# Gated mixer of a decoder trunk: the projection of r cut into pieces between the steps of the recurrent core

## The chip, the cores and the metric

The kernel runs on one core of a Trainium2 chip. The metric is the device time of one execution in microseconds (us). The engines are TensorE (PE, matmuls; PEld is its weight load), VectorE (DVE), ScalarE (ACT), GpSimd (POOL) and SyncE (SP), which here issues the weight transfers.

## The reference, cut to what matters

The program computes a two-layer decoder trunk on 512 tokens of width 1024. Each layer has a half feed-forward block, a token mixer, a cross attention to a fixed memory and a second half feed-forward block. The mixer of the second layer is a gated linear attention with four heads, keys of width 128 and values of width 256, in chunks of 64 tokens. The change touches this mixer alone.

```python
def gla_mixer(h, w_in, w_g2, b_g, head_norm, w_out):
    q, k, v, g_lr, r = _split(h @ w_in, ODD_SPLITS)
    gk = jax.nn.log_sigmoid((g_lr @ w_g2 + b_g)) / GLA_TAU
    ...
    q_dec = q * jnp.exp(G)
    k_inv = k * jnp.exp(-G)
    k_rem = k * jnp.exp(G_last - G)
    att = jnp.where(tril, jnp.einsum('bnhid,bnhjd->bnhij', q_dec, k_inv), 0.0)
    o_intra = jnp.einsum('bnhij,bnhjv->bnhiv', att, v)

    def step(state, xs):
        qd, kr, vv, dec = xs
        o = jnp.einsum('bhid,bhdv->bhiv', qd, state)
        state = dec[..., None] * state + jnp.einsum('bhjd,bhjv->bhdv', kr, vv)
        return state, o
    ...
    o = rmsnorm(o, head_norm).reshape(Bb, S, GLA_DV) * jax.nn.silu(r)
    return o @ w_out
```

## The kernel before, in words

All weights stream through one queue in units of 128 x 1024 elements. SyncE loads a unit into one of two raw buffers (w_raw). ScalarE copies it to the rounded high half w_hi (split_hi, L305), and VectorE subtracts to get the low half w_lo (split_lo, L310). Four slots hold split units. The order of these splits is written out by hand: behind unit u of a projection stands the split of unit u + 4 (AHEAD). A projection of one unit is 8 blocks of 3 matmuls of 512 columns (three, L325 to L327): high by high, high by low, low by high.

In the mixer (gla), TensorE projects g_lr, q, k and v, in this order. The gates are worked out on ScalarE and VectorE beside the projection of v, head by head. For each head n VectorE then forms g_q, g_kr (the keys that decay to the chunk's end, L1300) and g_k, and TensorE turns g_kr by four transposes a head (the keys' turns, L1693). ScalarE copies them out to g_krt (L834). Then TensorE projects r in 8 units. Behind each, ScalarE takes the bank through Silu into g_r (L645) and splits a coming unit, whose low half VectorE forms.

Then comes the core, 16 steps w: four groups T of 128 tokens by four heads n. A step on TensorE has these parts:

- att: 128 x 128 scores into bank w % 2 (L1725), which VectorE copies out under a mask (g_att, L1311)
- u: two products of keys and values of 64 rows each (L1731), from which VectorE updates the state g_S (L1320, L1322)
- mixed(w - 1): the output of the step before, from g_att and g_S (L1710, L1716). ScalarE copies it to f (L842) and sums its squares (L845)

At the last head of a group ScalarE takes a root (L849, it needs the Sqrt table), and VectorE's mean and normed scale the group before (L1337 to L1349). Behind the core TensorE turns f (L1742), VectorE multiplies it by g_r (gated, L1361), ScalarE and VectorE split the product (L854, L1366), and the output projection (L1492 to L1494) starts when all of it is there.

The banks of u are what decides how far TensorE may run ahead of VectorE's state updates; before the change there are two pairs of them:

```python
                        new, up = g_S[:, n, (c + 1) % 3, :], bank(2 + 4 * a + w % 2)[:, 0:GDV]
```

Of the kernel before, what the change touches and what calls it, by code (L numbers as in the profile page):

```python
# [60 lines left out]
def trunk(nc, parts, x, mem, wstream, cols, gains, post_gains, mem_gains, head_gain, w_ra, w_ri, w_g2, out):  # L61
# [7 lines left out]
    with ctx:  # L69
# [92 lines left out]
        def bank(b):  # L162
            return ps[:, b, :]
# [121 lines left out]

        def proj_bank(i, t):

            first = PT0[i, UNITS[parts[i][0]][0][0]]
            return bank(t - first if parts[i][0] in ("even", "gla") and t - first in (2, 3) else t % 2)

        VG = {"ffn": 0, "cross": 2, "even": 1, "gla": 2}
        V0 = [sum(VG[k] for k, _, _ in parts[:i]) for i in range(NP)]
# [154 lines left out]
        def _(act):  # L447
# [344 lines left out]
            def gla(i):  # L792
                nc.scalar.dma_start(g_w2[:, :], w_g2).then_inc(gs["w2_in"], 16)
                nc.scalar.dma_start(g_gain[:, :], head_gain.to_broadcast([P, GDV])).then_inc(gs["gain_in"], 16)
                act.preload_act_table_set("natural_log_exp_and_others")
                act.wait_ge(w_free, U[i, "g_lr"] + 3)
                nc.scalar.activation(g_lr[:, :], bank(PT0[i, "g_lr"] % 2)[0:GR, :], ACT.Copy).then_inc(p_free, 1)
                split_units(i, "g_lr", 1)
                project(i, "q", GH, g_q)
                for n in range(GH):  # L800
                    c = COLS["b_g"] + n
                    act.wait_ge(gs["z_full"], n + 1)
                    nc.scalar.activation(g_kr[:, n, :], bank(4 + n), ACT.Identity, bias=col[:, c:c + 1])\
                        .then_inc(gs["z"], 1)
                project(i, "k", GH, g_k)
                act.wait_ge(p_free, PT0[i, "k"] + GH + 2)
                act.preload_act_table_set("natural_log_exp_and_others")
                for n in range(GH):

                    split_units(i, "v", 1, 2 * n)  # L810
                    act.wait_ge(gs["z"], n + 1)
                    if n > 0:
                        act.wait_ge(gs["G"], 2 * n)
                    nc.scalar.activation(tmp[:, 0, :], g_kr[:, n, :], ACT.Abs).then_inc(gs["abs"], 1)
                    act.wait_ge(gs["abs"], n + 1)
# [12 lines left out]
                    nc.scalar.activation(tmp[:, 3, :], tmp[:, 3, :], ACT.Exp, scale=1.0 / 16).then_inc(gs["e"], 1)  # L828
                    split_units(i, "v", 1, 2 * n + 1)
                act.wait_ge(w_free, U[i, "v"] + 10)  # L830
                nc.scalar.activation(g_v[:, :, SEQ:2 * SEQ], ps[:, 0:4, :], ACT.Copy).then_inc(v_ready, 1)
                for n in range(GH):
                    act.wait_ge(gs["krT"], n + 1)
                    nc.scalar.activation(g_krt[:, :, n, :], bank(4 + n).rearrange("p (t c) -> p t c", t=TT), ACT.Copy)\  # L834
                        .then_inc(gs["krt"], 1)
                act.preload_act_table(ACT.Silu)
                project(i, "r", KT, g_r, func=ACT.Silu)
                act.preload_act_table(ACT.Sqrt)
                for w in range(TT * GH):
                    T, n = w // GH, w % GH  # L840
                    act.wait_ge(gs["o_full"], w + 1)
                    nc.scalar.activation(f[:, T, n * GDV:(n + 1) * GDV], bank(4 + w % 2)[:, 0:GDV], ACT.Copy)  # L842
                    if w > 0:
                        act.wait_ge(gs["osq"], w)
                    nc.scalar.activation(tmp[:, 2, 0:GDV], bank(4 + w % 2)[:, 0:GDV], ACT.Square,  # L845
                                         accum_out=g_st[:, 0, w:w + 1]).then_inc(gs["osq"], 1)
                    if n == GH - 1:
                        act.wait_ge(gs["osq"], w + 1)
                        nc.scalar.activation(g_st[:, 3, GH * T:GH * (T + 1)], g_st[:, 0, GH * T:GH * (T + 1)],  # L849
                                             ACT.Sqrt, scale=1.0 / GDV, bias=eps[:, 0:1]).then_inc(gs["root"], 1)  # L850
                for T in range(TT):
                    for b in range(2):
                        act.wait_ge(gs["y"], 2 * T + b + 1)
                        nc.scalar.activation(x_hi[:, 4 * b:4 * b + 4, T * P:(T + 1) * P],  # L854
                                             tmp[:, 2 * (T % 2) + b, :].rearrange("p (k c) -> p k c", k=4), ACT.Copy)\
                            .then_inc(gs["y_hi"], 1)
                output(i, "out", KT // 2)
# [16 lines left out]
        def _(dve):  # L874
# [193 lines left out]
            def project(i, seg, n):  # L1068
                split_units(i, seg, n)
# [203 lines left out]
            def gla(i):  # L1273
# [4 lines left out]
                for n in range(GH):  # L1278
# [20 lines left out]
                                                   ALU.mult, ALU.mult).then_inc(gs["qk"], 1)  # L1299
                    nc.vector.tensor_tensor(z, g_k[:, n, :], tmp[:, 3, :], ALU.mult).then_inc(gs["qk"], 1)  # L1300
                    nc.vector.tensor_tensor(g_k[:, n, :], g_k[:, n, :], g_t[:, 1, :], ALU.mult).then_inc(gs["qk"], 1)
                project(i, "r", KT)
                dve.wait_ge(gs["qk"], 3 * GH)
                dve.wait_ge(gs["zero"], 1)
                dve.wait_ge(gs["mask"], 3)
                for w in range(TT * GH):
# [7 lines left out]
                    for a in range(2):  # L1314
                        c = 2 * T + a
                        if c == SEQ // CH - 1:
                            break
                        new, up = g_S[:, n, (c + 1) % 3, :], bank(2 + 4 * a + w % 2)[:, 0:GDV]
                        if c == 0:
                            ins = nc.vector.tensor_copy(new, up)  # L1320
                        else:
                            ins = nc.vector.scalar_tensor_tensor(new, g_S[:, n, c % 3, :], g_dec[:, n, c:c + 1], up,  # L1322
                                                                 ALU.mult, ALU.add)
                        link(ins) if a == 0 and c != SEQ // CH - 2 else ins.then_inc(gs["S"], 1)
                    if w % GH == GH - 1 and T > 0:
                        mean(T - 1)
                        normed(T - 1)
# [56 lines left out]
        def _(pe):  # L1384
# [289 lines left out]
            def gla(i):  # L1674
# [12 lines left out]
                values(i, "v", 1, 4, 4, x_hi, x_lo, TT, 0)  # L1687
                pe.wait_ge(v_ready, V0[i] + 1)

                for n in range(GH):  # L1690
                    pe.wait_ge(gs["qk"], 3 * n + 2)
                    for t in range(TT):
                        last = nc.tensor.transpose(bank(4 + n)[:, t * P:(t + 1) * P], g_kr[:, n, t * P:(t + 1) * P],  # L1693
                                                   ident[:, :])
                    last.then_inc(gs["krT"], 1)
                pe.wait_ge(v_ready, V0[i] + 2)
                project(i, "r", KT, x_hi, x_lo)
                pe.wait_ge(gs["krt"], GH)
                pe.wait_ge(p_free, PT0[i, "r"] + KT + 2)
                pe.wait_ge(gs["qk"], 3 * GH)  # L1700

                def mixed(w):
# [17 lines left out]
                for w in range(TT * GH + 1):  # L1720
                    if w < TT * GH:
                        T, n = w // GH, w % GH
                        if w >= 2:
                            pe.wait_ge(gs["att"], w - 1)
                        nc.tensor.matmul(bank(w % 2)[:, 0:P], g_k[:, n, T * P:(T + 1) * P], g_q[:, n, T * P:(T + 1) * P],  # L1725
                                         start=True, stop=True).then_inc(gs["att_full"], 1)
                        if w >= 2:
                            pe.wait_ge(gs["S"], w - 1)
                        for a in range(2):
                            rows = slice(a * CH, (a + 1) * CH)  # L1730
                            last = nc.tensor.matmul(bank(2 + 4 * a + w % 2)[:, 0:GDV], g_krt[rows, T, n, :],  # L1731
                                                    g_v[rows, T, n * GDV:(n + 1) * GDV], start=True, stop=True)
                        last.then_inc(gs["u_full"], 1)
                    if w >= 1:
                        mixed(w - 1)
                for T in range(TT):
# [106 lines left out]
```

## Time and profile before

| what | value |
|---|---|
| median of 3 runs | 2441.12 us |
| lowest and highest run | 2437.56 and 2442.05 us |
| the profiled execution, its own time | 2437.72 us |
| its span, first to last instruction | 2435.0 us |
| TensorE busy, share of the span | 96% |
| VectorE, ScalarE busy | 43%, 34% |
| mean granted TensorE clock | 0.970 |

The mixer's part that changes runs from 1722 to 1825 us in the profiled execution. A busy share of 96% for TensorE says little by itself, since it is a mean over stages; what matters is where the chain of work that ended last leaves TensorE.

### The profile page before, as it was taken

Reading aid. Unit: us, or ns where it says so; the run is one execution under the profiler, and the core shown is the slowest. Engines: PE = TensorE matmul, PEld = TensorE weight load, DVE = VectorE, ACT = ScalarE, POOL = GpSimd, SP = SyncE. Lnnn points to the kernel's source line nnn. Section 1 sums busy time; section 2 is a strip of 40 time slices with the busy share of each in tenths; the row PEclk is TensorE's granted clock in tenths of the full one; section 3 lists DMA queues with packets and bytes.
Section 4 is the critical chain, followed back from the end, with each engine's and each line's share of the span. In section 5 each row is a group of like instructions: output and inputs, shape, how many; then the busy total and the mean of one; then the engine's idle time right before and its main releaser. Section 6 shows DMA issues by size and latency. Waiting matters only on the chain.

```text
span 2435.0 us, 28758 instructions
## 1 busy us (share of the span) xinstructions
PE 2332.7 (96%) x10808; PEld 1883.4 (77%) x10808; DVE 1038.3 (43%) x1608; ACT 835.3 (34%) x1311; POOL 48.0 (2%) x54
## 2 busy tenths in 40 slices
PE   7999999997898899999999999999989999999998
PEld 7888888573487588888888888887747867888887
DVE  4333235697553453333253333243364444433322
ACT  4222224353253343222243232243434434322321
POOL 0000000330000000000000000000000000000000
PEclk9999999796899999999999999999999999999999
DMA  4333332120134123333323333332203412233332
GB/s 156 95 95 96 111 114 81 35 78 18 52 113 125 40 84 106 96 96 110 96 87 104 102 96 104 96 92 93 86 27 112 147 61 78 87 95 95 95 103 86
DMA packets 61937, 221.81 MB, mean 91 GB/s; under 512 B 7952, under 2 KB 8080, under 8 KB 61856
## 3 DMA queue, kind: packets, MB, share of 16 engines
q1 hardware_dynamic: 57024, 207.64, 27.1%
q10 hardware_dynamic: 4832, 13.03, 1.6%
q8 instruction: 58, 0.95, 0.2%
q14 instruction: 23, 0.19, 0.0%
HBM read 218.55 MB, written 2.10 MB: 91 GB/s over the span
## 4 chain that ended last, share of the span: by engine, by line
PE 88%; DVE 8%; issue 2%; ACT 1%; DMA 0%; SPq 0%; DVEq 0%; ACTq 0%
PE ps L325 17%; PE ps L326 17%; PE ps L327 17%; PE ps L1492 10%; PE ps L1494 10%; PE ps L1493 10%; DVE e_sc L1210 1%; PE ps L1587 1%; DVE e_max L1209 1%; PE ps L1664 1%; PE ps L1395 1%; DVE w_lo L310 1%; PE ps L1623 1%; PE ps L1578 1%; PE ps L1656 0%
## 5 line engine op out<-in xcount | busy, mean ns | idle before, releaser
L325 PE MATMUL ps<-x_hi,w_hi 128*128 128x512 f32 (+1 forms) x2016 | 750.1, 372 | 12.9 <-issue 10.7
L326 PE MATMUL ps<-x_lo,w_hi 128*128 128x512 f32 (+1 forms) x2016 | 747.7, 371 | 0.0
L327 PE MATMUL ps<-x_hi,w_lo 128*128 128x512 f32 (+1 forms) x2016 | 747.1, 371 | 0.0
L310 DVE TENSOR_TENSOR w_lo<-w_raw,w_hi 128x1024 fp32r<-128x1024 f32 x196 | 245.2, 1252 | 558.4 <-ACT w_hi L305 557.4
L325 PEld LDWEIGHTS ps<-x_hi,w_hi 128*128 128x128 f32 x2016 | 383.0, 190 | 81.7 <-issue 17.2
L327 PEld LDWEIGHTS ps<-x_hi,w_lo 128*128 128x128 f32 x2016 | 382.7, 190 | 64.7
L326 PEld LDWEIGHTS ps<-x_lo,w_hi 128*128 128x128 f32 x2016 | 382.9, 190 | 63.9 <-issue 0.2
L305 ACT ACTIVATE w_hi<-w_raw 128x1024 fp32r<-128x1024 f32 x196 | 207.2, 1057 | 400.8 <-PE ps L1494 319.0
L321 DVE TENSOR_TENSOR w_lo<-w_raw,w_hi 128x1024 fp32r<-128x1024 f32 x176 | 215.8, 1226 | 291.8 <-ACT w_hi L316 291.8
L316 ACT ACTIVATE w_hi<-w_raw 128x1024 fp32r<-128x1024 f32 x176 | 186.2, 1058 | 282.1 <-PE ps L327 276.4
L1492 PE MATMUL ps<-w_hi,act_hi 128*128 128x512 f32 x608 | 236.5, 389 | 0.0
L1493 PE MATMUL ps<-w_lo,act_hi 128*128 128x512 f32 x608 | 236.5, 389 | 0.0
L1494 PE MATMUL ps<-w_hi,act_lo 128*128 128x512 f32 x608 | 236.5, 389 | 0.0
L1014 DVE TENSOR_TENSOR tmp<-ps,tmp 128x512 f32<-128x512 f32 x88 | 60.8, 691 | 314.9 <-ACT tmp L578 314.9
L578 ACT ACTIVATE tmp<-ps 128x512 f32<-128x512 f32 x88 | 52.8, 600 | 369.9 <-PE ps L327 369.9
L1493 PEld LDWEIGHTS ps<-w_lo,act_hi 128*128 128x128 f32 x608 | 114.1, 188 | 23.7
L1492 PEld LDWEIGHTS ps<-w_hi,act_hi 128*128 128x128 f32 x608 | 114.1, 188 | 23.7
L1494 PEld LDWEIGHTS ps<-w_hi,act_lo 128*128 128x128 f32 x608 | 114.1, 188 | 23.7
L1492 PE MATMUL ps<-w_hi,x_hi 128*128 128x512 f32 x272 | 107.5, 395 | 8.8 <-DVE x_lo L1366 4.5
L1493 PE MATMUL ps<-w_lo,x_hi 128*128 128x512 f32 x272 | 106.7, 392 | 0.0
L1494 PE MATMUL ps<-w_hi,x_lo 128*128 128x512 f32 x272 | 106.6, 392 | 0.0
L1492 PEld LDWEIGHTS ps<-w_hi,x_hi 128*128 128x128 f32 x272 | 51.6, 190 | 21.7 <-DVE x_lo L1085 6.1
(263 smaller groups left out, 2171.8 us busy)
## 6 DMA issues: line engine op xcount, KB each, us to landing
w_raw<-in_wstream SPq DMA_DIRECT2D x390, 512.0 KB, 3.6
gain_bc<-in_gains ACTq DMA_DIRECT2D x8, 512.0 KB, 4.6
tmp<-in_post_gains ACTq DMA_DIRECT2D x8, 512.0 KB, 4.4
c_mem<-in_mem ACTq DMA_DIRECT2D x2, 1024.0 KB, 5.4
out_dram<-h SPq DMA_DIRECT2D x4, 512.0 KB, 2.6
h<-in_x SPq DMA_DIRECT2D x2, 512.0 KB, 6.1
h<-in_x ACTq DMA_DIRECT2D x2, 512.0 KB, 7.5
c_gain<-in_mem_gains ACTq DMA_DIRECT2D x2, 512.0 KB, 6.7
```

The costliest lines, as they stand in the source:

```text
L305: nc.scalar.activation(weights(v)[0], w_raw[:, v % 2, :], ACT.Copy).then_inc(w_hi_ready, 1)
L310: nc.vector.tensor_tensor(wl, w_raw[:, v % 2, :], wh.bitcast(f32), ALU.subtract).then_inc(w_ready, 1)
L316: nc.scalar.activation(weights(like)[0], w_raw[:, like % 2, :], ACT.Copy).then_inc(w_hi_ready, 1)
L321: nc.vector.tensor_tensor(wl, w_raw[:, like % 2, :], wh.bitcast(f32), ALU.subtract).then_inc(w_ready, 1)
L325: nc.tensor.matmul(dst, wh, xh, start=start, stop=False)
L326: nc.tensor.matmul(dst, wh, xl, start=False, stop=False)
L327: return nc.tensor.matmul(dst, wl, xh, start=False, stop=stop)
L578: nc.scalar.activation(tmp[:, jj, :], bank(2 * jj), ACT.Silu).then_inc(silu_ready, 1)
L1014: nc.vector.tensor_tensor(tmp[:, jj, :], bank(2 * jj + 1), tmp[:, jj, :], ALU.mult)\
L1492: nc.tensor.matmul(dst, ah, wh, start=start, stop=False)
L1493: nc.tensor.matmul(dst, ah, wl, start=False, stop=False)
L1494: return nc.tensor.matmul(dst, al, wh, start=False, stop=stop)
```

## The change: what it does

The keys' turns move behind the first two units of r (R_FIRST = 2). They write banks 0 to 3, where they wrote 4 to 7. The other six units of r, 48 blocks, run inside the core, three blocks a step (R_BLOCKS = 3), between u and mixed(w - 1). Units of r alternate between banks 6 and 7. So the core's u products keep one pair of banks, 2 and 3, and the u of step w waits for the state update of step w - 1, where it waited for that of w - 2. The Silu of unit j, and the splits that follow a unit, stand in steps 2, 5, 7, 10, 13 and 15 of the core for j = 2 to 7 (r_done).

```diff
         def proj_bank(i, t):
 
+            if parts[i][0] == "gla" and t >= PT0[i, "r"]:
+                return bank(6 + (t - PT0[i, "r"]) % 2)
...
+        R_FIRST, R_BLOCKS = 2, 3
+        r_done = {(UB * (j + 1 - R_FIRST) - 1) // R_BLOCKS: j for j in range(R_FIRST, KT)}
...
+                act.preload_act_table(ACT.Silu)
+
+                def gate(j):
+                    act.wait_ge(w_free, U[i, "r"] + j + 3)
+                    nc.scalar.activation(g_r[:, j, :], proj_bank(i, PT0[i, "r"] + j), ACT.Silu).then_inc(p_free, 1)
+                    split_hi(act, U[i, "r"] + j + AHEAD)
+
+                for j in range(R_FIRST):
+                    gate(j)
                 for n in range(GH):
                     act.wait_ge(gs["krT"], n + 1)
-                    nc.scalar.activation(g_krt[:, :, n, :], bank(4 + n).rearrange("p (t c) -> p t c", t=TT), ACT.Copy)\
+                    nc.scalar.activation(g_krt[:, :, n, :], bank(n).rearrange("p (t c) -> p t c", t=TT), ACT.Copy)\
                         .then_inc(gs["krt"], 1)
-                act.preload_act_table(ACT.Silu)
-                project(i, "r", KT, g_r, func=ACT.Silu)
-                act.preload_act_table(ACT.Sqrt)
...
+                for step in range(TT * GH + 1):
+                    w = step - 1
...
+                    if step in r_done:
+                        gate(r_done[step])
...
-                project(i, "r", KT)
+                for j in range(R_FIRST):
+                    split_lo(dve, U[i, "r"] + j + AHEAD)
...
-                        new, up = g_S[:, n, (c + 1) % 3, :], bank(2 + 4 * a + w % 2)[:, 0:GDV]
+                        new, up = g_S[:, n, (c + 1) % 3, :], bank(2 + a)[:, 0:GDV]
...
+                    if w in r_done:
+                        split_lo(dve, U[i, "r"] + r_done[w] + AHEAD)
                     if w % GH == GH - 1 and T > 0:
                         mean(T - 1)
                         normed(T - 1)
...
+                for n in range(R_FIRST * UB):
+                    gate(n)
+                pe.wait_ge(v_ready, V0[i] + 2)
...
-                        if w >= 2:
-                            pe.wait_ge(gs["S"], w - 1)
+                        if w >= 1:
+                            pe.wait_ge(gs["S"], w)
...
+                        for n in range(R_BLOCKS * w, R_BLOCKS * (w + 1)):
+                            gate(R_FIRST * UB + n)
```

**TensorE, one step of the core.** From mixed(1) to the u of step 3 the queue before the change reads as follows (ps is the accumulation memory; L1710 and L1716 are mixed, L1725 is att, L1731 is u):

```order
L1710 MATMUL ps<-g_v,g_att 128x256 [waits g_S,g_att]
L1716 MATMUL ps<-g_S,g_q 64x256
L1725 MATMUL ps<-g_q,g_k 128x128 [waits g_att]
L1731 MATMUL ps<-g_v,g_krt 128x256 [waits g_S]
L1731 MATMUL ps<-g_v,g_krt 128x256
```

With the change this stands on the same engine from the att of step 2 to its last piece of r (L1759 is att, L1765 is u, L330 to L332 are the three matmuls of a block):

```order
L1759 MATMUL ps<-g_q,g_k 128x128 [waits g_att]
L1765 MATMUL ps<-g_v,g_krt 128x256 [waits g_S]
L1765 MATMUL ps<-g_v,g_krt 128x256
L330 MATMUL ps<-x_hi,w_hi 128x512
L331 MATMUL ps<-x_lo,w_hi 128x512
L332 MATMUL ps<-x_hi,w_lo 128x512
L330 MATMUL ps<-x_hi,w_hi 128x512
L331 MATMUL ps<-x_lo,w_hi 128x512
L332 MATMUL ps<-x_hi,w_lo 128x512
L330 MATMUL ps<-x_hi,w_hi 128x512 [waits w_ready,p_free]
L331 MATMUL ps<-x_lo,w_hi 128x512
L332 MATMUL ps<-x_hi,w_lo 128x512
```

Nine matmuls of r stand between u and the mixed that follows, and a new unit of r begins at the third block.

**ScalarE, the end of the core.** Before the change the last two steps read so (f and tmp are mixed's copy and square, L849 is the root):

```order
L842 ACTIVATE f<-ps 128x256 [waits g_o_full]
L845 ACTIVATE tmp,g_st<-ps 128x256 [waits g_osq]
L842 ACTIVATE f<-ps 128x256 [waits g_o_full]
L845 ACTIVATE tmp,g_st<-ps 128x256 [waits g_osq]
L849 ACTIVATE g_st<-g_st,eps 128x4 [waits g_osq]
```

With the change ScalarE's queue from step 13 to the root of the last group is this (L841 is the Silu of a unit of r, L310 the split of a weight unit, L855 and L858 the copy and the square):

```order
L841 ACT_TABLE_LOAD
L841 ACTIVATE g_r<-ps 128x512 [waits w_free]
L310 ACTIVATE w_hi<-w_raw 128x1024 [waits w_free,w_in0]
L855 ACTIVATE f<-ps 128x256 [waits g_o_full]
L858 ACTIVATE tmp,g_st<-ps 128x256 [waits g_osq]
L855 ACTIVATE f<-ps 128x256 [waits g_o_full]
L858 ACTIVATE tmp,g_st<-ps 128x256 [waits g_osq]
L841 ACTIVATE g_r<-ps 128x512 [waits w_free]
L310 ACTIVATE w_hi<-w_raw 128x1024 [waits w_free,w_in1]
L855 ACTIVATE f<-ps 128x256 [waits g_o_full]
L858 ACTIVATE tmp,g_st<-ps 128x256 [waits g_osq]
L862 ACT_TABLE_LOAD
```

The Silu and the split of units 6 and 7 have moved in between the copies, and the engine changes its table before unit 6 and before the last root. In the whole core there are seven such loads: four ahead of a root and three ahead of a Silu.

## Rows read from the trace of the kernel before

**Rows 1.** The page, part 4: shares of the chain that ended last, by engine.
```profile
PE 88%; DVE 8%; issue 2%; ACT 1%; DMA 0%; SPq 0%; DVEq 0%; ACTq 0%
```

**Rows 2.** Busy time by stretch: start:end, length, engines, PEclk, DMA share, GB/s.
```profile
1726.00:1735.00 9.00, 7.03 (x27) 5.87 (x28) 2.52 (x5) 4.48 (x6) 0.00 (x0) 0.81 0.18 58
```

**Rows 3.** Timeline around the keys' turns: start, length, engine, line, instructions, [wait].
```profile
1722.30 1.47 PE L1693 MATMUL ps<-ident,g_kr 128*128 128x128 f32 x12
...
1725.29 1.85 ACT L831 ACTIVATE g_v<-ps 128x2048 f32<-128x2048 f32 x1
...
1727.04 1.56 ACT L834 ACTIVATE g_krt<-ps 128x512 f32<-128x512 f32 x3
...
1727.97 1.11 PE L1693 MATMUL ps<-ident,g_kr 128*128 128x128 f32 x4 [4.20 <-DVE g_kr L1300]
```

**Rows 4.** The chain that ended last, at the start of r's projection.
```profile
1729.08 0.43 PE ps L325
...
1730.79 0.36 PE ps L326
```

**Rows 5.** Timeline of ScalarE and VectorE in r's projection, first unit and last.
```profile
1735.54 0.60 ACT L645 ACTIVATE g_r<-ps 128x512 f32<-128x512 f32 x1 [4.52 <-PE ps L327]
1736.03 1.05 ACT L305 ACTIVATE w_hi<-w_raw 128x1024 fp32r<-128x1024 f32 x1
...
1737.12 1.23 DVE L310 TENSOR_TENSOR w_lo<-w_raw,w_hi 128x1024 fp32r<-128x1024 f32 x1 [8.60 <-ACT w_hi L305]
...
1773.62 0.60 ACT L645 ACTIVATE g_r<-ps 128x512 f32<-128x512 f32 x1 [3.89 <-PE ps L327]
```

**Rows 6.** Timeline of TensorE at the start of the core.
```profile
1774.32 0.46 PE L1725 MATMUL ps<-g_q,g_k 128*128 128x128 f32 x2 [0.73 <-issue]
...
1777.61 0.67 PE L1710 MATMUL ps<-g_v,g_att 128*128 128x256 f32 x2 [1.15 <-DVE g_S L1322]
```

**Rows 7.** The chain that ended last, in one step of the core.
```profile
1804.14 0.63 PE ps L1731 x4
1804.78 0.63 PE ps L1710 x2
1805.40 0.58 PE ps L1716 x4
1805.99 0.42 PE ps L1725 x2
```

**Rows 8.** Timeline of ScalarE behind that step.
```profile
1806.58 0.20 ACT L845 ACTIVATION_READ_ACCUMULATOR tmp<-ps 128x1 f32 x1
```

**Rows 9.** Timeline of VectorE behind steps 7 to 9 of the core.
```profile
1792.17 0.16 DVE L1337 TENSOR_SCALAR g_st<-g_st 128x4 f32<-128x4 f32 x1
...
1794.36 0.29 DVE L1311 COPY_PREDICATED g_att<-g_mask,ps 128x128 f32<-128x128 int32 x1
1794.56 0.99 DVE L1322 SCALAR_TENSOR_TENSOR g_S<-g_S,g_dec,ps 128x256 f32<-128x256 f32 x2
1795.47 0.29 DVE L1311 COPY_PREDICATED g_att<-g_mask,ps 128x128 f32<-128x128 int32 x1
```

**Rows 10.** Timeline around the core's end.
```profile
1809.86 0.65 PE L1716 MATMUL ps<-g_S,g_q 128*64 128x256 f32 x4
...
1814.76 1.28 DVE L1361 TENSOR_TENSOR tmp<-ps,g_r 128x512 f32<-128x512 f32 x2
```

**Rows 11.** Timeline of ScalarE in the even mixer, where it changes its table.
```profile
431.46 0.38 ACT L738 ACTIVATE tmp<-ps 128x256 f32<-128x256 f32 x1 [0.92 <-PE ps L1623]
431.87 1.28 ACT L727 ACT_TABLE_LOAD   x1
433.16 0.63 ACT L727 ACTIVATE e_t<-tmp 128x512 f32<-128x512 f32 x1
```

**Rows 12.** Matmuls of one line (lengths, first and last start), and one behind them.
```profile
L1648 PE MATMUL ps<-e_xc,e_bd x16: 590/592/592, 514.4 to 520.8; 128*128 128x512 f32 x16
...
521.47 0.40 PE L326 MATMUL ps<-x_lo,w_hi 128*128 128x512 f32 x1
```

More of the change, by code:

```diff
@@ L833, in gla @@
                     act.wait_ge(gs["krT"], n + 1)
-                    nc.scalar.activation(g_krt[:, :, n, :], bank(4 + n).rearrange("p (t c) -> p t c", t=TT), ACT.Copy)\
+                    nc.scalar.activation(g_krt[:, :, n, :], bank(n).rearrange("p (t c) -> p t c", t=TT), ACT.Copy)\
                         .then_inc(gs["krt"], 1)
-                act.preload_act_table(ACT.Silu)
-                project(i, "r", KT, g_r, func=ACT.Silu)
-                act.preload_act_table(ACT.Sqrt)
[L839 to L850, printed above, removed]
@@ new lines, in gla @@
+                for step in range(TT * GH + 1):
+                    w = step - 1
+                    if w >= 0:
+                        T, n = w // GH, w % GH
+                        act.wait_ge(gs["o_full"], w + 1)
+                        nc.scalar.activation(f[:, T, n * GDV:(n + 1) * GDV], bank(4 + w % 2)[:, 0:GDV], ACT.Copy)
+                        if w > 0:
+                            act.wait_ge(gs["osq"], w)
+                        nc.scalar.activation(tmp[:, 2, 0:GDV], bank(4 + w % 2)[:, 0:GDV], ACT.Square,
+                                             accum_out=g_st[:, 0, w:w + 1]).then_inc(gs["osq"], 1)
+                        if n == GH - 1:
+                            act.wait_ge(gs["osq"], w + 1)
+                            nc.scalar.activation(g_st[:, 3, GH * T:GH * (T + 1)], g_st[:, 0, GH * T:GH * (T + 1)],
+                                                 ACT.Sqrt, scale=1.0 / GDV, bias=eps[:, 0:1]).then_inc(gs["root"], 1)
+                    if step in r_done:
+                        gate(r_done[step])
@@ L1688, in gla, with gate @@
                 pe.wait_ge(v_ready, V0[i] + 1)
+                r0 = PT0[i, "r"]
+                def gate(n):
+                    j, b = divmod(n, UB)
+                    u = U[i, "r"] + j
+                    wh, wl = weights(u)
+                    if b == 0:
+                        pe.wait_ge(p_free, r0 + j + 1)
+                        pe.wait_ge(w_ready, u + 1)
+                    at = slice(b * P, (b + 1) * P)
+                    last = three(proj_bank(i, r0 + j), wh[:, at], wl[:, at], x_hi[:, b, :], x_lo[:, b, :],
+                                 b == 0, b == UB - 1)
+                    if b == UB - 1:
+                        last.then_inc(w_free, 1)
+                for n in range(R_FIRST * UB):
+                    gate(n)
+                pe.wait_ge(v_ready, V0[i] + 2)
                 for n in range(GH):
@@ L1692, in gla @@
                     for t in range(TT):
-                        last = nc.tensor.transpose(bank(4 + n)[:, t * P:(t + 1) * P], g_kr[:, n, t * P:(t + 1) * P],
+                        last = nc.tensor.transpose(bank(n)[:, t * P:(t + 1) * P], g_kr[:, n, t * P:(t + 1) * P],
                                                    ident[:, :])
                     last.then_inc(gs["krT"], 1)
-                pe.wait_ge(v_ready, V0[i] + 2)
-                project(i, "r", KT, x_hi, x_lo)
                 pe.wait_ge(gs["krt"], GH)
-                pe.wait_ge(p_free, PT0[i, "r"] + KT + 2)
                 pe.wait_ge(gs["qk"], 3 * GH)
@@ L1726, in gla @@
                                          start=True, stop=True).then_inc(gs["att_full"], 1)
-                        if w >= 2:
-                            pe.wait_ge(gs["S"], w - 1)
+                        if w >= 1:
+                            pe.wait_ge(gs["S"], w)
                         for a in range(2):
                             rows = slice(a * CH, (a + 1) * CH)
-                            last = nc.tensor.matmul(bank(2 + 4 * a + w % 2)[:, 0:GDV], g_krt[rows, T, n, :],
+                            last = nc.tensor.matmul(bank(2 + a)[:, 0:GDV], g_krt[rows, T, n, :],
                                                     g_v[rows, T, n * GDV:(n + 1) * GDV], start=True, stop=True)
                         last.then_inc(gs["u_full"], 1)
+                        for n in range(R_BLOCKS * w, R_BLOCKS * (w + 1)):
+                            gate(R_FIRST * UB + n)
                     if w >= 1:
```

## Prediction

> **What bounds the kernel now.** I read the page first. The chain that ended last lies on TensorE for 88% [rows 1], so only what moves TensorE's work, or the handover between stages, can move the time. Then I followed that chain and the timeline through the mixer, from the end of v (1722.3 us) to the first product with g_r. Three places there are not TensorE's own work.
>
> First, the keys' turns. Twelve of the 16 transposes run at once, 1.47 us or 0.12 each. The last four wait 4.20 us for VectorE's g_kr of the last head [rows 3]. In that wait the granted clock falls: 0.81 over the 9 us around it [rows 2], which is part of the time at 1.2 GHz and the rest at 2.4. The four take 1.11 us where 0.49 is the pace of the twelve, and five matmuls of r come every 0.43 us [rows 3, 4]. The pace of r follows from its first and last Silu, 38.08 us apart for seven units of 24 matmuls: 0.227 each [rows 5]. That is 0.6 + 5 x 0.2 = 1.6 us for the clock, and 5.8 with the wait.
>
> Second, the entry of the core. r's last matmul is done by 1773.4 (its Silu starts at 1773.62), the first mixed starts at 1777.61 [rows 5, 6]. Between them TensorE has two times att and u, 2 x (0.42 + 0.63) = 2.1 us of work [rows 7], so 2.1 are lost.
>
> Third, the end. The core itself is TensorE's own work back to back, 0.63 + 0.63 + 0.58 + 0.42 = 2.26 us a step [rows 7]. Mixed(14) ends at 1809.86 + 0.65 = 1810.51, and gated starts at 1814.76, 4.25 later [rows 10]. From there VectorE is the bound.
>
> **The change part by part.** The most it can give back on TensorE is 5.8 + 2.1 = 7.9 us; no matmul is removed or added.
>
> *The turns behind two units.* These units take 16 blocks x 3 x 0.227 = 10.9 us and start at once, since the first four units of r are split beside v. At 1733.2 all of g_kr has long been there, and 16 transposes take 1.96 to 1735.2. But what follows them is now ScalarE. Its g_v copy ends at 1727.1 [rows 3], and the table for Silu with the first unit's work are hidden behind the second unit. The second unit's Silu can start only at 1733.4; 0.49 later the split, 1.05 long [rows 5], so ScalarE is free at 1734.9. Four copies of the turned keys at the pace of three in 1.56 us [rows 3] take 2.0, to 1736.9. TensorE waits 1736.95 - 1735.2 = 1.75 us. The core starts at 1736.95.
>
> *A step of the core with r.* TensorE: 2.26 + 9 x 0.227 = 4.30 us, and 3.09 for step 0, which has no mixed. A switch between the two kinds of matmul is not shown at these sizes. The nearest rows are 16 matmuls of 512 columns between others of r's kind: they start 0.427 apart (514.4 to 520.8, 15 intervals), so the second one behind them is due at 520.8 + 0.43 + 0.23 = 521.46, and it starts at 521.47: nothing lost [rows 12]. Below lies a gain: a 256-column matmul's weight load shows as 0.1 us beside its stream (0.63 for two passes against 0.43), and one of them could hide behind r, -0.1. Above, a switch may show such a load too, +0.2 for two. I take 0.04, near the row but for the short columns here on the side of the loss: 16 x 0.04 = 0.6 us, bounds -1.6 and +3.2.
>
> *The wait for the state.* With one pair of banks the u of step w + 2 waits for the state update of w + 1. In the six steps that end a unit, that update stands behind a chain. From the end of mixed(w - 1), ScalarE needs 0.79 for copy and squares (PE ends at 1805.98, the last read at 1806.78) [rows 7, 8], 0.49 for the Silu, 1.05 for the split [rows 5]. VectorE's low half takes 1.15 to its next start (1.23 less an overlap of 0.08), then 0.20 to the state and 0.99 for it [rows 5, 9]. With 0.10 for the handovers the sum is 4.77. TensorE wants it after a step and an att, 4.30 + 0.42 = 4.72. So, in tenths:
> - step 2's chain: 0.1 lost.
> - step 5's: a table load in front of the Silu, as the root of step 4 took the engine to Sqrt. A load is 1.28 and the next instruction follows it at once [rows 11]: 1.3 lost.
> - step 7's: no load, but mean and normed stand behind the split, 1792.17 to 1794.36 = 2.2 us [rows 9]: 2.3 lost.
> - step 10's: a load, 1.3. Step 13's: a load, but one state update in place of two from group 3 on, 0.8.
> These are 5.8 us. In the other steps VectorE has a 4.30 us step for its 1.1 or 3.3 us and nobody waits.
>
> Of this sum the table is the part for which the notes have another number. The Trainium skill (page "ScalarE: Activation LUTs", section "What ACT_TABLE_LOAD costs") puts a switch at 1.28 us plus a drain of 1.38. Here 431.46 + 0.38 = 431.84 is followed by the load at 431.87, and its user starts at 433.16 [rows 11]; no drain shows.
>
> *The end.* Step 15 ends the last unit. VectorE does not go on to normed(2) behind its last state, as it did; it waits for the split. From the end of mixed(14): 0.79 + 0.49 + 1.05 + 0.03 + 1.15 = 3.5, then normed(2) and normed(3), 2.2 each [rows 9]: gated starts 7.9 us behind it, where it was 4.25 [rows 10]: 3.65 later. The load before the last root (ready at about 4.6) lies under normed(2). Behind gated nothing is changed; each later step keeps its length, and the weight queue is four units ahead as before.
>
> *The sum.* Mixed(14) ends at 1736.95 + 3.09 + 15 x 4.30 + 5.8 = 1810.3, as before within 0.2: the 7.9 saved are spent as 1.75 + 5.8. Gated starts at 1810.3 + 7.9 = 1818.2, 3.5 us later than 1814.76. With 0.6 for switches, +4.1. The profiled execution takes 2437.7 us by its own time, so 2441.8 there. That execution lies 3.4 below the median of the three runs, 2441.1, and the median of the changed kernel should be 2445.2, or 2445.
>
> **The rivals.** A measurement of this kernel tells 0.2% (4.9 us) from no change; the forecast, +4.1, is just inside.
> - *The clock falls inside the new stages* (slower). The transposes, the wait of 1.75 us and the first att and u leave TensorE thin for 4.8 us; the waits of 2.3 and 1.3 us come next. For it: it fell in a wait of 4.20 [rows 3]. Against it: at the old entry of the core 4.2 us with half of them idle (1773.4 to 1777.61) left the pace of a step at 2.26 [rows 6, 7]. A fall costs ten matmuls of r at 0.43, twice the five of rows 4: +2.0, so +6.1, 2447.
> The page "TensorE: Matmul & The Clock Gate" of the Trainium skill (section "The HAM clock gate") has the clock run in just two states, set by recent activity; the 0.81 of rows 2 agrees as a mixture of them.
> - *The switches cost their weight loads* (slower): +3.2 for +0.6, so +6.7, 2448. It decides from 0.09 us a step.
> - *Each table switch costs twice its load* (slower): a drain as long as the load adds 1.3 in three steps, +3.9, so 2449. Rows 11 speak against it.
> - *The splits hide* (no change). If ScalarE loads its table while it waits for mixed, the waits fall by 3 x 1.3: +0.2, 2441. The load stands behind the copy in its queue, which speaks against it.
> - *r covers the core's weight loads* (faster). Each 128 or 256-column pass shows 0.1 us of load; where r streams before it, it may hide. One mechanism, up to 0.8 us a step; in the ten steps that no chain bounds that is -8, so -3.9 in all, 2437. It crosses to faster only from 0.9 us a step, or with the splits hidden too. Rows 12 show no gain.
>
> **How the numbers follow.** Forecast 0.48, the clock 0.22, the switches 0.13, the table 0.04, hidden splits 0.07, covered loads 0.06. Slower by over 0.2% are the clock, the switches and the table, and a small part of the forecast's own spread (+2 to +6): 0.42. Faster keeps 0.05, as the covered loads barely reach it. The rest, 0.53, is the same. The range goes from the covered loads, 2437 with a part of that case left out, to the clock and the switches together (4.1 + 2.0 + 2.6 = +8.7, 2450) and a second fall, 2452: 2438 to 2452.
>
> **What would show it.** In the changed profile: the last transposes with no wait before them and no fall of the clock; a wait of 1.75 us of L1759 on ScalarE's g_krt; u (L1765) waiting for VectorE's g_S after steps 5, 7, 10 and 13, by 1.3, 2.3, 1.3 and 0.8 us; seven loads of 1.28 us in the core; gated (L1379) 7.9 us after the end of mixed(14), at about 1818. I would be wrong if u waits nowhere, if a step without a chain takes other than 4.3 us, or if the clock falls between 1733 and 1812.

## The result, and the profile after

The changed kernel takes 2445.56 us (median of 15 runs, 2439.27 to 2449.52), the kernel before 2439.67 us (15 runs beside them). The ratio is 1.0023 with a 95% interval of 1.0014 to 1.0032: 3.4 to 7.8 us slower. Six more runs of it, told below, came out 8.2 us above theirs. In the profiled execution the span is 2440.0 us, before 2435.0.

The page alone would show nothing of it. Its part 4 (the chain that ended last, by engine) reads as [rows 1] did:

```profile
PE 88%; DVE 8%; issue 2%; ACT 1%; DMA 0%; SPq 0%; DVEq 0%; ACTq 0%
```

So the stage has to be timed from its own rows, from the first instruction behind v to the first product with g_r. Before it took 1814.76 - 1722.30 = 92.5 us [rows 3, 10]. First the timeline of TensorE around the keys' turns (L330 is r, L1730 the turns, L1759 the first att):

```profile
1724.39 0.39 PE L330 MATMUL ps<-x_hi,w_hi 128*128 128x512 f32 x1
...
1735.27 1.91 PE L1730 MATMUL ps<-ident,g_kr 128*128 128x128 f32 x16
1739.02 0.49 PE L1759 MATMUL ps<-g_q,g_k 128*128 128x128 f32 x2 [1.83 <-ACT g_krt L848]
```

r follows v at once, and the turns follow r with no wait, where four of them stood 4.20 us behind the others [rows 3]. The wait has a new owner: 1.83 us on ScalarE's g_krt. Then the timeline of TensorE in the core, the four places where u (L1765) waits for the state:

```profile
1769.97 0.70 PE L1765 MATMUL ps<-g_v,g_krt 64*128 64x256 f32 x4 [1.31 <-DVE g_S L1338]
...
1780.84 0.70 PE L1765 MATMUL ps<-g_v,g_krt 64*128 64x256 f32 x4 [2.09 <-DVE g_S L1338]
...
1795.27 0.70 PE L1765 MATMUL ps<-g_v,g_krt 64*128 64x256 f32 x4 [1.31 <-DVE g_S L1338]
...
1809.15 0.70 PE L1765 MATMUL ps<-g_v,g_krt 64*128 64x256 f32 x4 [0.79 <-DVE g_S L1338]
```

They sum to 5.50 us; before there was one wait in the core, at its entry [rows 6]. What the first of them waits for is to be read from the timeline of ScalarE and VectorE in step 5:

```profile
1764.50 0.20 ACT L858 ACTIVATION_READ_ACCUMULATOR tmp<-ps 128x1 f32 x1
1764.72 1.28 ACT L841 ACT_TABLE_LOAD   x1
1766.01 0.60 ACT L841 ACTIVATE g_r<-ps 128x512 f32<-128x512 f32 x1
1766.51 1.05 ACT L310 ACTIVATE w_hi<-w_raw 128x1024 fp32r<-128x1024 f32 x1
...
1767.59 1.22 DVE L315 TENSOR_TENSOR w_lo<-w_raw,w_hi 128x1024 fp32r<-128x1024 f32 x1 [5.92 <-ACT w_hi L310]
1768.73 0.29 DVE L1327 COPY_PREDICATED g_att<-g_mask,ps 128x128 f32<-128x128 int32 x1
1768.93 0.99 DVE L1338 SCALAR_TENSOR_TENSOR g_S<-g_S,g_dec,ps 128x256 f32<-128x256 f32 x2
```

Each starts where the one above it ends: squares, table load, Silu, split of a weight unit, its low half on VectorE, and only then g_att and g_S of step 6. And the timeline around the core's end:

```profile
1813.08 0.70 PE L1744 MATMUL ps<-g_v,g_att 128*128 128x256 f32 x2
...
1813.83 0.60 ACT L841 ACTIVATE g_r<-ps 128x512 f32<-128x512 f32 x1
1814.31 1.07 ACT L310 ACTIVATE w_hi<-w_raw 128x1024 fp32r<-128x1024 f32 x1
...
1815.40 1.22 DVE L315 TENSOR_TENSOR w_lo<-w_raw,w_hi 128x1024 fp32r<-128x1024 f32 x1 [5.02 <-ACT w_hi L310]
...
1816.55 0.16 DVE L1355 TENSOR_SCALAR g_st<-g_st 128x4 f32<-128x4 f32 x1
...
1818.74 0.16 DVE L1355 TENSOR_SCALAR g_st<-g_st 128x4 f32<-128x4 f32 x1
...
1820.94 1.28 DVE L1379 TENSOR_TENSOR tmp<-ps,g_r 128x512 f32<-128x512 f32 x2
```

Mixed(14) ends where mixed(15) starts, at 1813.08, and gated (L1379) starts at 1820.94, 7.86 us later; before it was 4.25 [rows 10]. VectorE stands idle until its half of the split at 1815.40, then does normed(2) (from 1816.55) and normed(3) (from 1818.74).

The stage takes 1820.94 - 1724.39 = 96.5 us, 4.1 more than before. The span grew by 5.0. The rest lies outside the stage, where the program is the same (v ended 2.1 us later in this execution, and 1.2 came back behind gated). That part scatters: over the 13 profiles of this document v ends between 1716.9 and 1726.2 us, and 618.9 to 624.1 us follow behind the start of gated. The stage of one kernel repeats to 0.1 us where the clock does the same in it (turns only, turns and entry, twice each below), so the parts of the change are read from the stage.

### The profile page after: what moved, and what is told of

Read it like the earlier page. It is cut to its first block, busy times and chain, and to the rows that moved or that the text cites. A ratio compares the mean times of both kernels' runs of the same rounds, so it can differ in the third digit from the quotient of the medians.

```text
span 2440.0 us, 28764 instructions
## 1 busy us (share of the span) xinstructions
PE 2335.6 (96%) x10808; PEld 1884.4 (77%) x10808; DVE 1037.3 (43%) x1608; ACT 842.1 (35%) x1317; POOL 47.9 (2%) x54
## 4 chain that ended last, share of the span: by engine, by line
PE 88%; DVE 8%; issue 2%; ACT 1%; DMA 0%; SPq 0%; DVEq 0%; ACTq 0%
PE ps L330 17%; PE ps L332 17%; PE ps L331 17%; PE ps L1510 10%; PE ps L1511 10%; PE ps L1512 10%; PE ps L1605 1%; DVE e_sc L1225 1%; DVE e_max L1224 1%; PE ps L1682 1%; PE ps L1413 1%; DVE w_lo L315 1%; PE ps L1641 1%; PE ps L1596 1%; PE ps L1674 0%
## 5 line engine op out<-in xcount | busy, mean ns | idle before, releaser
L330 PE MATMUL ps<-x_hi,w_hi 128*128 128x512 f32 (+1 forms) x2016 | 751.8, 373 | 11.7 <-issue 9.6
L332 PE MATMUL ps<-x_hi,w_lo 128*128 128x512 f32 (+1 forms) x2016 | 747.3, 371 | 0.0
L330 PEld LDWEIGHTS ps<-x_hi,w_hi 128*128 128x128 f32 x2016 | 382.9, 190 | 84.7 <-issue 20.9
L332 PEld LDWEIGHTS ps<-x_hi,w_lo 128*128 128x128 f32 x2016 | 382.8, 190 | 64.5
L310 ACT ACTIVATE w_hi<-w_raw 128x1024 fp32r<-128x1024 f32 x196 | 207.2, 1057 | 398.9 <-PE ps L1512 318.4
```

Of the source, the lines that this page charges most:

```text
L310: nc.scalar.activation(weights(v)[0], w_raw[:, v % 2, :], ACT.Copy).then_inc(w_hi_ready, 1)
L330: nc.tensor.matmul(dst, wh, xh, start=start, stop=False)
L332: return nc.tensor.matmul(dst, wl, xh, start=False, stop=stop)
```

## The experiments

Each kernel is told by the length of its stage, as above, by its waits, and by the ratio to the kernel before. A profile is one execution, so a second number matters: the falls of TensorE's granted clock inside the stage, which are told with the change run again, below.

| kernel | stage, us | falls in it | ratio to before (95%) |
|---|---|---|---|
| before | 92.5 | 1 | |
| the change | 96.5 | 0 | 1.0023 (1.0014 to 1.0032) |
| the change again | 98.3 | 1 | 1.0033 (1.0021 to 1.0045) |
| turns only | 86.7 | 0 | 0.9964 (0.9950 to 0.9978) |
| turns only again | 86.6 | 0 | 0.9967 (0.9955 to 0.9979) |
| gate first | 91.1 | 1 | 0.9994 (0.9982 to 1.0006) |
| split late | 94.5 | 1 | 1.0012 (1.0002 to 1.0021) |
| no loads | 96.0 | 2 | 1.0014 (1.0005 to 1.0024) |
| turned keys first | 97.3 | 1 | 1.0020 (1.0008 to 1.0032) |
| all remedies | 87.7 | 0 | 0.9981 (0.9969 to 0.9992) |
| turns and entry | 84.6 | 0 | 0.9978 (0.9967 to 0.9988) |
| turns and entry again | 84.6 | 0 | 0.9969 (0.9957 to 0.9980) |
| one pair of banks | 102.1 | 2 | one run, 2450.22 us |

### The turns alone

Against the changed kernel:

```diff
+                for j in range(R_FIRST, KT):
+                    gate(j)
+                act.preload_act_table(ACT.Sqrt)
...
-                        for n in range(R_BLOCKS * w, R_BLOCKS * (w + 1)):
-                            gate(R_FIRST * UB + n)
```

The core's banks, waits and VectorE's splits are those of the kernel before.

> One half of the change alone: the keys' turns behind the first two units of r, with the changed kernel's banks, but units 2 to 7 of r in front of the core as before, and the core with its two pairs of banks and no split in it. Theory (the 7.9 us that the change saves on TensorE are spent on waits for ScalarE's and VectorE's splits inside the core): here they are kept where the turns are concerned. The wait of 4.2 us and the half clock are gone, the copies of the turned keys lie under unit 2, the entry of the core still loses its 2.1 us. From the first instruction behind v to gated the stage takes 92.5 - 5.8 = 86.7 us (before 92.5, changed kernel 96.6), so about 5.8 us faster than before, 0.24%. Rival (the turns' wait was only ahead of a wait that comes anyway, so the clock or the copies give it back): the stage takes 90 us or more.

Measured: 86.7 us, and 9 us below before in the medians (2430.66 against 2439.70 us). The timeline shows the turns at once and the copies of the turned keys, which now nobody waits for:

```profile
1733.52 1.91 PE L1729 MATMUL ps<-ident,g_kr 128*128 128x128 f32 x16
...
1735.16 2.06 ACT L848 ACTIVATE g_krt<-ps 128x512 f32<-128x512 f32 x4
```

So the half of the change that moves the turns is worth its 5.8 us in the stage, and the half that cuts r into pieces, with its one pair of banks, costs about 10: it takes the stage from 86.7 to 96.5. The 9 us of the medians are more than the stage shows, but their interval (5.4 to 12.2 us) holds 5.8. The rival falls.

### The gate ahead of the copy

```diff
                 for step in range(TT * GH + 1):
                     w = step - 1
+                    if step in r_done:
+                        gate(r_done[step])
...
-                    if step in r_done:
-                        gate(r_done[step])
```

> The changed kernel, but ScalarE's Silu and split of a unit stand ahead of the copy of mixed in the same step, not behind it. TensorE ends the unit before mixed, so the split ends 2.0 us earlier and the Silu's table is loaded while ScalarE is idle. Theory: three of the four waits of u on the state (1.2, 2.1, 1.2 and 0.7 us measured) vanish, that behind step 7 falls to 0.4; gated starts 6.1 us behind mixed(14) and not 7.9. The stage from v to gated takes 96.6 - 6.7 = 89.9 us, 2.6 less than before. Rival (the waits come from the single pair of banks as such, not from what stands in ScalarE's queue): the waits stay within 0.3 us each and the stage takes about 96.

(The expectations of this group quote the waits as 1.2, 2.1, 1.2 and 0.7 us, from a sum; the rows above have 1.31, 2.09, 1.31 and 0.79.) Measured: 91.1 us, and one wait of u where there were four. The timeline of TensorE has these two waits in the whole stage behind v:

```profile
1736.27 0.49 PE L1759 MATMUL ps<-g_q,g_k 128*128 128x128 f32 x2 [1.83 <-ACT g_krt L848]
...
1776.58 0.70 PE L1765 MATMUL ps<-g_v,g_krt 64*128 64x256 f32 x4 [0.42 <-DVE g_S L1338]
```

The core still has its one pair of banks, and three waits are gone. ScalarE now loads the table for Silu in the time in which it waited for mixed (timeline of ScalarE in step 5, L857 is the copy):

```profile
1760.79 1.28 ACT L841 ACT_TABLE_LOAD   x1
1762.09 0.60 ACT L841 ACTIVATE g_r<-ps 128x512 f32<-128x512 f32 x1
...
1763.53 0.38 ACT L857 ACTIVATE f<-ps 128x256 f32<-128x256 f32 x1
```

So it is the place in ScalarE's queue that makes them. The stage is 1.2 us longer than expected: the clock fell once behind the wait for g_krt.

### The low half behind normed

```diff
-                    if w in r_done:
-                        split_lo(dve, U[i, "r"] + r_done[w] + AHEAD)
                     if w % GH == GH - 1 and T > 0:
                         mean(T - 1)
                         normed(T - 1)
+                    if w in r_done:
+                        split_lo(dve, U[i, "r"] + r_done[w] + AHEAD)
```

> The changed kernel, but VectorE's low half of the split stands behind mean and normed in steps 7 and 15, not ahead of them. Theory: the wait behind step 7 vanishes (2.1 us), as VectorE does normed in the time in which it waited for the split; the others stay (1.2, 1.2, 0.7). In the end gated starts 6.4 us behind mixed(14), bound by ScalarE's root behind its table load, and not 7.9. The stage takes 96.6 - 3.6 = 93.0 us. Rival (VectorE's work is simply too much for the stage, in any order): the wait behind step 7 only moves to another step, and the stage stays within 1 us of 96.6.

Measured: 94.5 us with a fall of the clock behind the wait for g_krt, which is 1.5 more than expected. The waits of u are now these (timeline of TensorE):

```profile
1773.35 0.70 PE L1765 MATMUL ps<-g_v,g_krt 64*128 64x256 f32 x4 [1.31 <-DVE g_S L1338]
...
1796.43 0.70 PE L1765 MATMUL ps<-g_v,g_krt 64*128 64x256 f32 x4 [1.31 <-DVE g_S L1338]
...
1810.32 0.70 PE L1765 MATMUL ps<-g_v,g_krt 64*128 64x256 f32 x4 [0.80 <-DVE g_S L1338]
```

The one of 2.09 us behind step 7 is gone and has not moved elsewhere; the core's last output product starts 5.5 us ahead of gated, and 7.0 in the changed kernel. VectorE's work fits; its order did not.

### No table loads

```diff
-                    nc.scalar.activation(g_r[:, j, :], proj_bank(i, PT0[i, "r"] + j), ACT.Silu).then_inc(p_free, 1)
+                    nc.scalar.activation(g_r[:, j, :], proj_bank(i, PT0[i, "r"] + j), ACT.Silu if j < R_FIRST else ACT.Copy)\
+                        .then_inc(p_free, 1)
```

> The changed kernel, but units 2 to 7 of r are copied out without Silu, so the gate is not the reference's for them and ScalarE keeps one table from the first root on. Theory: the loads of 1.28 us in front of the Silu in steps 5, 10 and 13 are what the waits of u there are made of: 1.2, 1.2 and 0.7 us vanish, the one behind step 7 (2.1, normed) stays. The load before the last root goes too, but it is hidden. The stage takes 96.6 - 3.2 = 93.4 us. Rival (a switch costs the load and a drain as long): more than 3.2 us, 6 or so, would go, up to 90.5 us.

Measured: one wait of u is left, the one behind step 7:

```profile
1779.15 0.75 PE L1766 MATMUL ps<-g_v,g_krt 64*128 64x256 f32 x4 [2.09 <-DVE g_S L1339]
```

5.50 - 2.09 = 3.4 us of waits went with three loads of 1.28 us (the last of these waits had only been 0.79). The stage took 96.0 us all the same, as the clock fell twice in it, behind the wait for g_krt and behind this one. From the first att to the start of the last output product the core took 74.4 us, 75.0 in the changed kernel: 3.4 less and 2.8 more.

### The change again, and what the clock does

> The changed kernel once more, unchanged. Its first profile showed no fall of the clock inside the stage, while the profiles of three kernels with the same entry of the core (gate first, split late, no loads) show one each just behind the wait of 1.8 us on g_krt, and the last a second one behind the wait of 2.1 us. Theory: the clock falls there by chance, in about three executions of four, and costs 1.6 us, so this profile shows a stage of about 98.1 us with a fall at the core's entry, and the median stays 4 to 7 us above before. Rival (the fall belongs to those kernels): the stage takes 96.5 us again, with PEclk at 1.00 from v to gated.

Measured: 98.3 us, with the same waits within 0.01 us (1.83, then 5.5 in four). The windows view of the entry of the core (start:end, length, busy time of the engines, PEclk, DMA share, GB/s):

```profile
1731.00:1733.00 2.00, 0.24 (x2) 0.24 (x2) 1.02 (x1) 1.71 (x4) 0.00 (x0) 1.00 0.00 0
1733.00:1737.00 4.00, 4.00 (x14) 2.82 (x14) 1.20 (x3) 0.00 (x0) 0.00 (x0) 0.66 0.38 131
1737.00:1741.00 4.00, 4.00 (x19) 2.94 (x17) 1.21 (x3) 0.00 (x0) 0.00 (x0) 0.91 0.00 0
```

Behind the wait the clock stands at 0.50 for some 3.4 us (0.66 and 0.91 are means over four), that is at 1.2 GHz. The same kernel had 1.00 there in its first profile, whose first att stands at 1739.02:

```profile
1740.00:1741.00 1.00, 1.00 (x6) 0.80 (x5) 0.78 (x2) 0.00 (x0) 0.00 (x0) 1.00 0.89 344
1741.00:1742.00 1.00, 1.00 (x6) 0.81 (x5) 0.12 (x1) 0.00 (x0) 0.00 (x0) 1.00 0.21 82
```

Of the six profiles with the pieces of r and a wait of 0.9 us or more at the entry and waits inside the core (the change twice, gate first, split late, no loads, turned keys first), five show a fall, one of them two. In the profile of all remedies, whose one wait is 0.90 us, it does not fall. A fall costs 1.3 to 1.7 us, read from the length of the core less its waits: 75.0 - 5.5 = 69.5 in the change, 76.7 - 5.5 = 71.2 when it was run again, 71.2 - 0.4 = 70.8 with the gate first, 74.3 - 3.4 = 70.9 with the split late.

The six runs have a median of 2448.13 us against 2439.92 for before, 8.2 more, where 4 to 7 were expected. Their interval, 5.1 to 11.0 us, holds the stage with a fall (+5.8) and not the one without (+4.1).

### The turned keys ahead of the split

```diff
                 for j in range(R_FIRST):
-                    gate(j)
+                    gate(j, j < R_FIRST - 1)
                 for n in range(GH):
...
+                split_hi(act, U[i, "r"] + R_FIRST - 1 + AHEAD)
```

> The changed kernel, but ScalarE's split behind the second unit of r stands behind the four copies of the turned keys, not ahead of them. Theory: TensorE's wait before the core is ScalarE's split of 1.05 us and the copies, so it falls from 1.8 to about 0.75 us; nothing else changes, and the stage takes 95.5 us without a fall of the clock, 97.1 with one. With the shorter wait the fall at the entry should become rare. Rival (the copies wait for the transposes or the bank, not for the split): the wait stays at 1.8 us.

Measured (timeline of ScalarE and TensorE):

```profile
1735.84 2.06 ACT L849 ACTIVATE g_krt<-ps 128x512 f32<-128x512 f32 x4
1737.74 1.09 ACT L310 ACTIVATE w_hi<-w_raw 128x1024 fp32r<-128x1024 f32 x1
...
1737.95 0.49 PE L1761 MATMUL ps<-g_q,g_k 128*128 128x128 f32 x2 [0.90 <-ACT g_krt L849]
```

The wait is 0.90 us where it was 1.83: the split took 0.93 of its 1.05. No fall stands at the entry in this profile, but one behind the wait of 2.09 us, which ended at 1779.91 (windows view):

```profile
1780.00:1781.00 1.00, 1.00 (x6) 0.62 (x7) 0.41 (x2) 0.00 (x0) 0.00 (x0) 1.00 0.00 0
1782.00:1783.00 1.00, 1.00 (x3) 0.73 (x3) 0.00 (x0) 0.00 (x0) 0.00 (x0) 0.50 0.00 0
```

So the stage took 97.3 us. That the shorter wait makes the fall rarer is not shown by one profile.

### All remedies, and the entry without pieces

The first takes three edits together, the gate first, the split late and the turned keys first, and loads the table for the last root behind the last unit of r.

> All remedies on the changed kernel together: gate ahead of the copy on ScalarE, the low half behind mean and normed on VectorE, the turned keys copied ahead of the split, and the table for the last root loaded behind the last unit. Theory: no u waits for the state, the wait before the core is 0.75 us, gated starts 5.4 us behind mixed(14); the stage takes 87.6 us, or 89.2 with one fall of the clock, so 3 to 5 us less than before and 1 us or more behind the turns alone (86.7), since there is nothing left for the pieces of r to hide but the 2.1 us of the entry. Rival (pieces between steps are the better form once they are well ordered): below 86 us.

Measured: 87.7 us in an execution without a fall, and medians 4.3 us apart (2435.67 against 2439.92). The timeline of TensorE has one wait from v to gated, and this is it:

```profile
1730.55 0.49 PE L1763 MATMUL ps<-g_q,g_k 128*128 128x128 f32 x2 [0.90 <-ACT g_krt L849]
```

That is 9 us less than the change, 5 less than before, and 1 more than the turns alone. The pieces of r, ordered well, harm little and show no gain over the plain order.

The second goes the other way: all of r stays in front of the core, and the entry is mended by itself.

Against the turns alone:

```diff
-                    gate(j)
+                    gate(j, j < KT - 1)
...
+                    if w == 3:
+                        split_hi(act, U[i, "r"] + KT - 1 + AHEAD)
...
+                    if w == 5:
+                        split_lo(dve, U[i, "r"] + KT - 1 + AHEAD)
...
-                pe.wait_ge(p_free, r0 + KT + 2)
...
+                        if w < 2:
+                            pe.wait_ge(p_free, r0 + KT + 1 + w)
```

> The turns alone, and beside them the entry of the core mended without any piece of r in it: the split behind r's last unit moves on ScalarE behind the root of step 3 of the core and on VectorE behind the state of step 5, and TensorE waits for the last bank of r only where u needs it, in step 1. Theory: of the 2.1 us lost at the entry 1.9 come back, the stage takes 84.8 us, 7.7 less than before, and the time falls by 0.3% or a little more. Rival (another wait stands behind the one removed, at the entry or in steps 5 to 7): the stage stays above 86.

Measured: 84.6 us. The timeline of TensorE at the entry:

```profile
1767.57 0.39 PE L332 MATMUL ps<-x_hi,w_lo 128*128 128x512 f32 x1
1767.80 0.38 PE L1765 MATMUL ps<-g_q,g_k 128*128 128x128 f32 x2
...
1769.94 0.67 PE L1750 MATMUL ps<-g_v,g_att 128*128 128x256 f32 x2
```

The first att follows r's last matmul by 0.23 us and the first mixed comes 2.1 us later without a wait; at [rows 6] it was 3.3 with a wait of 1.15 in it, and TensorE had stood 0.73 ahead of the att. In the runs this kernel was first 6.4 us below before and the turns alone 9.0, in the other order to their stages, so both were run again.

> The turns alone once more, unchanged, beside the turns with the mended entry on the same chip. In the two earlier jobs the first was 0.36% and the second 0.22% below before, though its stage is 2.1 us shorter (84.6 against 86.7). Theory: the stage is 86.7 us again, and the order of the two medians is scatter from falls of the clock elsewhere in the program; expected 5.8 us below before. Rival (the mended entry costs something outside the stage): the turns alone stay 2 us or more below the other.

> The turns with the mended entry once more, unchanged. Theory: a stage of 84.6 us again, 7.9 less than before, and the time 6 to 9 us below before and at or below that of the turns alone. Rival as there.

Measured: stages of 86.6 and 84.6 us again, medians 2431.92 and 2431.82 us against 2439.20. Neither rival shows: the turns alone are not 2 us below the other. Both versions beat the kernel before, by 0.22 to 0.36% in the four comparisons, and so the changed kernel too. That the mended entry adds its 2.1 us to the turns is shown in the stage and not in the run times, whose scatter (2428.2 to 2435.2 us for the two) is wider than that.

### One pair of banks by itself

Against the kernel before:

```diff
-bank(2 + 4 * a + w % 2)[:, 0:GDV]
+bank(2 + a)[:, 0:GDV]
...
-                        if w >= 2:
-                            pe.wait_ge(gs["S"], w - 1)
+                        if w >= 1:
+                            pe.wait_ge(gs["S"], w)
```

> The kernel before, but the core's u products have one pair of banks (2 and 3) and the u of step w waits for the state of step w - 1, as in the changed kernel; no piece of r is moved. Theory: without a split in the core one pair is nearly enough. VectorE's state takes 1.05 us behind u, and TensorE's next u is 1.6 us later. It costs 0.7 us at the entry (u of step 1 waits 1.8 us where mixed(0) waited 1.2) and 0.6 us behind normed in step 7; the stage takes 93.7 us against 92.5. Rival (one pair is what costs the changed kernel its time): 3 us or more.

Measured: the waits are near what was expected, 2.2 us in two places where before had 1.2 in one. The time is not: the stage took 102.1 us, 9.7 more than before and past the rival's bound of 3. The timeline, the waits view and the windows show why.

```profile
1780.16 0.49 PE L1725 MATMUL ps<-g_q,g_k 128*128 128x128 f32 x2
1782.34 1.22 PE L1731 MATMUL ps<-g_v,g_krt 64*128 64x256 f32 x4 [1.69 <-DVE g_S L1322]
1783.49 1.22 PE L1710 MATMUL ps<-g_v,g_att 128*128 128x256 f32 x2
```

```profile
PE ps L1731 <- DVE g_S L1322: 2.2, 2, 1.7
```

```profile
1781.00:1782.00 1.00, 0.00 (x0) 0.00 (x0) 0.96 (x4) 0.28 (x1) 0.00 (x0) 0.74 0.00 0
1781.00:1798.00 17.00, 15.66 (x39) 6.76 (x39) 6.04 (x16) 2.53 (x10) 0.00 (x0) 0.51 0.10 31
```

In the wait of 1.69 us, which ends at 1782.34, the clock falls, and the core runs at 1.2 GHz for 17 us: mixed's first product takes 1.15 us to the next start where it took 0.63. The other 1.2 us of the stage lie at the keys' turns, where the clock fell as before but for longer. So one pair of banks costs 1.0 us by its waits and, in this execution, some 7.5 us more by the clock. It is one execution, and no run says how often either fall happens or lasts so long.

## Why the prediction was right

**The sum.** The mechanism was right: what TensorE no longer waits for at the turns and the entry, it waits for ScalarE and VectorE inside the core, and the end of the core grows. Forecast +4.1 us in the stage, measured +4.1 (96.5 against 92.5) in an execution without a fall of the clock. The forecast median of 2445.2 stands beside 2445.56, but partly by chance: it was made from a median of before of 2441.12, which 15 runs put at 2439.67. The measured change of the medians is 5.9 us, 1.8 more than forecast. It lies just past the 0.2% that I had set as the bound of no change, to which I gave 0.53 against 0.42 for slower; its interval reaches to both sides of that bound. The second set of runs, +8.2 us with an interval from 5.1, lies past that bound and past +4.1.

**What each step measured.**

| step | forecast, us | measured, us |
|---|---|---|
| turns: wait and half clock gone | -5.8 | -5.8 (turns alone) |
| wait for g_krt | 1.75 | 1.83 |
| waits of u behind steps 2, 5, 7, 10, 13 | 0.1, 1.3, 2.3, 1.3, 0.8 | 0, 1.31, 2.09, 1.31, 0.79 |
| table load in each of three | 1.28 | 3.4 us of waits for three |
| mixed(14) to gated | 7.9 | 7.86 |
| switch between matmul kinds, a step | 0.04 | 0.04 |

**The switches.** The value was right and the bounds explain it. The chain that ended last, in step 3 of the changed core, shows both at once (L330 to L332 are r, L1744 is mixed):

```profile
1747.60 0.43 PE ps L330
1748.03 0.24 PE ps L331
1748.27 0.23 PE ps L332
...
1749.89 0.43 PE ps L1744 x2
```

The first matmul of r behind u takes 0.43 where its like take 0.23: a loss of 0.2, the upper bound. The first product of mixed behind r takes 0.43 where it took 0.63 [rows 7]: the gain that I had bounded at 0.1 is 0.2. The nearest row [rows 12] had shown nothing of either, so that the two cancel, and the 0.04 holds, is luck in part. A step that waits for nothing takes 4.34 us, for the 4.30 without switches. So the gain stands at the product right behind r and at no other, which is why the rival of the covered loads came to nothing. That it is the weight load that r covers is a reading and not shown.

**The rivals.** The clock was the one that mattered. Its chance of 0.22 looks too low: it fell in five profiles of six with such waits, and for the changed kernel itself in one of two. I had named a fall between 1733 and 1812 as a sign of being wrong; the first profile has none, the second has one, so the +4.1 holds for an execution without a fall and not for all. Its price, 2.0 us, was a little high against 1.3 to 1.7. Added to the sum it gives +5.4 to +5.8, which is inside the intervals of both sets of runs; that it is the whole of the missing 1.8 us is argued from profiles, not measured over all runs. The table's drain did not come: three loads took 3.4 us away with them, not twice that. Nor did the splits hide: the load starts at 1764.72, right behind the squares (1764.50 + 0.20), and not in the idle time before mixed. With the gate ahead of the copy it does start there, and three of the four waits go.

## What to carry to other kernels

When work is cut into pieces to fill waits on one engine, look at what follows each piece on the others: here a piece on TensorE trailed a table change, a copy and a split through ScalarE and VectorE, and these stood in front of the small steps that TensorE's next step needed. Put such service work ahead of a wait, or behind the urgent step, and sum its chain against the length of a step. And try the parts of a change apart: the move of the keys' turns was worth 5.8 us, and the interleaving beside it nothing that could be shown.

## What the runs showed of the hardware that was not expected

TensorE's clock fell behind a wait in one execution of the changed kernel and not in another, with the same waits. Over the six profiles named above, the wait of 1.83 us at the entry was followed by a fall in four of five and the one of 2.09 us in two of four; the waits of 0.79 to 1.31 us were followed by none. These falls lasted some 3.4 us and cost 1.3 to 1.7. In the kernel with one pair of banks a fall in a wait of 1.69 us lasted 17 us and cost some 7.5 (the core from its first att to its last output product took 45.5 us where it took 37.0 before, less the 1.0 of longer waits). What decides how long the clock stays at 1.2 GHz is not shown: at the keys' turns of that kernel it stayed there for 6.8 us, in the kernel before for 3.4, with the same instructions behind.

And a matmul in fp32 of 256 columns behind one of 512 takes 0.2 us less than behind its own kind (0.43 for 0.63), which a single switch the other way takes back (0.43 for 0.23).
